# Attention and FFN kernel for one core: work moved at the FFN entries and in the three-way attention

## The reference, cut to what matters

```
# first unit, twice
x = x + 0.5 * rmsnorm(swiglu(rmsnorm(x, g0), gate0, up0, down0), g1)
x = x + rmsnorm(token_mixer(rmsnorm(x, g2)), g3)
x = x + 0.5 * rmsnorm(swiglu(rmsnorm(x, g4), gate1, up1, down1), g5)
# second unit, twice (ALPHA = sqrt(2))
mix = concat(hgrn2(x), three_way_attention(x)) @ w_out
x = layer_norm(ALPHA * x + mix)
x = layer_norm(ALPHA * x + swiglu(x, gate, up, down))
```

## Time and profile before

| | |
|---|---|
| median of 3 runs | 3692.89 us (3686.24 to 3693.57) |
| the profiled execution | 3686.6 us, its span 3684.8 us |
| TensorE busy | 3502.5 us, 95% of the span |
| VectorE busy | 1686.9 us, 46% |
| ScalarE busy | 1272.8 us, 35% |
| GpSimd busy | 1418.8 us, 39% |
| mean granted TensorE clock | 0.980 |

### The profile page before, as it was taken

One profiled execution on the slowest core, in us unless ns is written; L12 is line 12 of the kernel. 1 busy time (PEld: TensorE's weight loads), 2 busy tenths in 40 slices (PEclk: granted clock), 3 DMA queues, 4 the chain that ended last, 5 costly groups with the idle time before them and its releaser, 6 DMA issues. The chain is left out here.

```text
span 3684.8 us, 45117 instructions
## 1 busy us (share of the span) xinstructions
PE 3502.5 (95%) x16116; PEld 2751.6 (75%) x16116; DVE 1686.9 (46%) x2604; ACT 1272.8 (35%) x2154; POOL 1418.8 (39%) x605
## 2 busy tenths in 40 slices
PE   7999999899989999999999999899999899889998
PEld 5888766688868887766788777557888777568886
DVE  5442344644244423255543346854331539753323
ACT  3222346422232223355222352453222442642223
POOL 3444321244434443322444434403444345124443
PEclk9999999999999999999999999999999999999999
DMA  4223311222222323211223231102323320112222
GB/s 150 97 96 100 108 63 41 69 97 97 94 79 97 97 96 110 75 46 52 91 97 97 86 122 53 46 18 81 97 95 99 110 76 29 41 50 95 95 96 98
DMA packets 86356, 307.15 MB, mean 83 GB/s; under 512 B 11173, under 2 KB 11813, under 8 KB 84942
## 3 DMA queue, kind: packets, MB, share of 16 engines
q1 hardware_dynamic: 86222, 305.38, 25.1%
HBM read 301.13 MB, written 4.21 MB: 83 GB/s over the span
## 5 line engine op out<-in xcount | busy, mean ns | idle before, releaser
L319 POOL TENSOR_TENSOR wL<-ring,wH 128x1024 fp32r<-128x1024 f32 (+1 forms) x525 | 1280.7, 2439 | 2147.3 <-ACT wH L309 2147.3
L273 PE MATMUL bank<-hH,wH 128*128 128x512 f32 x2448 | 966.7, 395 | 18.8 <-DVE guL L645 7.9
L275 PE MATMUL bank<-hH,wL 128*128 128x512 f32 x2448 | 954.3, 390 | 0.0
L274 PE MATMUL bank<-hL,wH 128*128 128x512 f32 x2448 | 954.0, 390 | 0.0
L309 ACT ACTIVATE wH<-ring 128x1024 fp32r<-128x1024 f32 (+1 forms) x525 | 551.0, 1050 | 1125.0 <-PE bank L275 945.0
L273 PEld LDWEIGHTS bank<-hH,wH 128*128 128x128 f32 x2448 | 460.3, 188 | 122.4 <-POOL wL L319 9.6
L275 PEld LDWEIGHTS bank<-hH,wL 128*128 128x128 f32 x2448 | 460.2, 188 | 97.2
L274 PEld LDWEIGHTS bank<-hL,wH 128*128 128x128 f32 x2448 | 460.7, 188 | 95.2 <-issue 2.4
L273 PE MATMUL bank<-guH,wH 128*128 128x512 f32 x1248 | 492.5, 395 | 2.3 <-ACT early L1141 1.4
L275 PE MATMUL bank<-guH,wL 128*128 128x512 f32 x1248 | 486.9, 390 | 0.0
L274 PE MATMUL bank<-guL,wH 128*128 128x512 f32 x1056 | 410.8, 389 | 0.0
(11 more groups left out here) (287 smaller groups left out, 4089.2 us busy)
## 6 DMA issues: line engine op xcount, KB each, us to landing
ring<-in_w SPq DMA_DIRECT2D x376, 512.0 KB, 3.3
ring<-in_down SPq DMA_DIRECT2D x96, 448.0 KB, 3.1
ring<-in_down SPq DMA_DIRECT2D x48, 512.0 KB, 3.3
ring<-in_next SPq DMA_DIRECT2D x16, 512.0 KB, 3.2
mix<-in_table SPq DMA_DIRECT2D x2, 2560.0 KB
mix<-bias SPq DMA_DIRECT2D x4, 768.0 KB, 5.6
ring<-in_vg SPq DMA_DIRECT2D x8, 280.0 KB, 2.9
xT<-in_xT SPq DMA_DIRECT2D x4, 512.0 KB, 6.6
```

Of the source, the lines that this page charges most:

```text
L273: eng.matmul(out, a, hi, start=first, stop=False)
L274: eng.matmul(out, a, lo, start=False, stop=False)
L275: return eng.matmul(out, b, hi, start=False, stop=last)
L319: eng.tensor_tensor(l[:, 0:width], ring[:, n % NSLOT, 0:width], h[:, 0:width], ALU.subtract).then_inc(w_lo, 1)
```

## The change

Three things change.

First, the fourth slot's low part at the first unit's stage entries (slot n0+3 of both FFNs and of the projections) goes from GpSimd to VectorE, behind the sum of squares (`vector_lo`, the old `third_lo`; the set `by_vector` takes GpSimd's part out). Second, `act_silu` makes the high part of slot n0+4 ahead of the root and of the Silu table, where it stood behind the first `silu`; and `hi` waits for the slot that really had its buffer (`buffer_before`), where it waited for the slot two before. This holds for the FFN of the second unit too. Third, in the three-way attention tile 0 of the out projection is taken and its mean made at step 1 (was 2), tile 1 is multiplied at step 2 (was 3), and `dve_early2` is cut in two: the scaling stays ahead of `post`, the centring and adding up (`dve_early2_mid`) go behind it.

```
+        by_vector = set()
+        def buffer_before(n):
+            n -= NSLOT
+            while n in spares or n in ahead:
+                n -= NSLOT
+            return n
...
         def hi(eng, n, width=WIDE, i=0, per=0):
...
-            if per or (n >= NSLOT and n not in spares and n not in ahead):
+            if per:
                 eng.wait_ge(slots_done, i * per + (n - NSLOT + 1))
+            elif n not in spares and n not in ahead and buffer_before(n) >= 0:
+                eng.wait_ge(slots_done, buffer_before(n) + 1)
...
         def lo(eng, n, width=WIDE, i=0, per=0):
-            if n >= total_slots[0] or per == 0 and n in spares and n > 2:
+            if n >= total_slots[0] or per == 0 and n in by_vector:
                 return
-            if per == 0 and n - 1 in spares and n > 3:
+            if per == 0 and n - 1 in by_vector:
                 eng.wait_ge(w_lo, n)
...
             hi(eng, n0 + 3)
+            hi(eng, n0 + 4)
             if stat is not None:
                 act_root(eng, stat, EPS_RMS)
             eng.preload_act_table(ACT.Silu)
-            for k in range(2):
-                silu(k)
-                hi(eng, n0 + 4 + k)
+            silu(0)
+            silu(1)
+            hi(eng, n0 + 5)
...
+        by_vector.update((3, n_in + 2, n_in + 3, n_ffn1 + 2, n_ffn1 + 3, n_next + 2))
...
                     sum_x_squares(dve, 0)
+                    vector_lo(dve, 3)
...
                     sum_x_squares(dve, 1)
+                    vector_lo(dve, n_in + 3)
...
                     sum_x_squares(dve, 2)
+                    vector_lo(dve, n_ffn1 + 3)
...
-                if u == 2:
+                if u == 1:
                     eng.wait_ge(early_out, 1)
                     eng.matmul(bank[7][:, :], onesD, early2(0), start=True, stop=True).then_inc(mean_out, 1)
...
-        EARLY2_AT = (3, 6, 7, 10, 11, 14, 15)
+        EARLY2_AT = (2, 6, 7, 10, 11, 14, 15)
...
         def dve_early2(eng, m):
...
-            if m == 0:
-                return
+
+        def dve_early2_mid(eng, m):
+
             if m == 1:
                 eng.wait_ge(mean_kept, 1)
...
-                if u == 2:
-                    dve_early2(eng, 0)
                 if u - 2 in EARLY2_AT:
                     dve_early2(eng, EARLY2_AT.index(u - 2) + 1)
                 if 1 <= u <= NU:
                     post(u - 1)
+                if u == 1:
+                    dve_early2(eng, 0)
+                if u - 2 in EARLY2_AT:
+                    dve_early2_mid(eng, EARLY2_AT.index(u - 2) + 1)
...
+                if u == 2:
+                    act_guess(eng)
                 if 1 <= u <= NU:
                     back(u - 1)
-                if u == 3:
-                    act_guess(eng)
```

More of the change, by code:

```diff
@@ L420, in moved, with vector_lo @@
                 eng.tensor_scalar(xT[:, m, :], yT[:, m, :], b[:, m:m + 1], None, ALU.add).then_inc(x_ready, 1)
-        def third_lo(eng, n):
+        def vector_lo(eng, n):
             eng.wait_ge(w_hi, n + 1)
@@ L440, in dve_post @@
                     rest(eng, h0, m - 1, gains)
-            third_lo(eng, third)
+            vector_lo(eng, third)
         def pair_of(eng, n, h0, banks=(0, 2)):
@@ L2329, in build @@
         spares.update((2, n_ffn2 + 2, n_next2 + 2))
+        by_vector.clear()
+        by_vector.update((n_ffn2 + 2, n_next2 + 2))
         ahead.clear()
```

## The result

The changed kernel takes 3668.72 us (median of 6 runs, 3667.52 to 3671.4), the kernel before 3688.29 us beside it (6 runs, 3685.26 to 3693.57). The ratio is 0.9948, 95% interval 0.9938 to 0.9958: 19.6 us or 0.52% faster. The forecast was 3681 us within 3673 to 3690, a gain of 10.3 us.

What follows compares the result with a forecast made beforehand. TensorE, busy for 95% of the span, was taken as the bound, so only its stops could be won: FFN entries 5.9 us plus attention 4.4 us gave 10.3 us, and 3681 us was forecast, range 3673 to 3690.

Steps and rivals of the forecast that it cites:

- FFN entries, 5.9 us: First unit's four FFN entries: TensorE's 7.9 us stop behind the first gate result shrinks; 6.7 us gained less 0.8.
- 0.55 us late: FFN entries: VectorE's added low part ends at about 709.87, while slot n0+3 began at 709.34, so that slot starts later.
- The 0.8 us set aside for L1376: Two first FFN entries: GpSimd's part may come ahead of L1376, delaying the gates; 0.8 us taken between nothing and 2.0.
- The landing that a rival spoke of: FFN entries of both units: slot n0+4's late load holds ScalarE ahead of the root; slower, 3699 us, chance 0.05.
- The reduction: Rival: without GpSimd's low part beside it the reduction shortens, up to 2.4 us in five of six places; 3669 us, chance 0.03.
- The second unit's entries: High part of slot n0+4 ahead of the table moves the first `silu` 3.5 us later, covered by TensorE's slots; cost zero.
- The loop's start, 0.3 us a layer lost: Attention steps 1 to 4: score reads 2.25 us late, TensorE level after turn 2 and tile 1, 0.3 us lost at step 4.
- the race that the prediction left open: Attention step 4, `post(4)` against GpSimd's low part: VectorE first wins 1.05 us, GpSimd first loses 0.5; 0.3 lost taken.
- The cut, 2.5 us a layer: Three-way attention: cutting `dve_early2` brings `post` 1.4 us sooner at steps 7, 11 and 15; gain 2.5 us per layer.
- the three waits behind `post`, 2.7 us: Attention: TensorE waits at `turn_cmp` for `post` three times per layer, 2.7 us together, the longest 1.6.
- theory C: From the follow-up runs' expectations: much of the gain is granted clock; entries alone 8 to 12 us less, attention alone 10 to 14.

Runs made afterwards that it cites:

- the second profile: The changed kernel run once more, unaltered, beside the kernel before: 3671.88 us, ratio 0.9954; its profiled execution took 3675.0 us.
- e1: Kernel before with the FFN entries part alone (high part of slot n0+4 early, low part of n0+3 on VectorE), attention as before: 3679.51 us, ratio 0.9974.
- e3: Kernel before with only the high part of slot n0+4 ahead of the root; low part of n0+3 stays on GpSimd: 3679.67 us, ratio 0.9974.
- e9: The changed kernel without the shift of the attention's start, so the entries part and the cut, against the kernel before: 3663.16 us, ratio 0.9932.
- e4: Kernel before with only the low part of slot n0+3 on VectorE; high part of n0+4 stays behind the first `silu`: 3688.1 us, ratio 0.9997.
- e5: Kernel before with only the cut of `dve_early2`; mean, tile 1 and guess at their old steps: 3670.0 us, ratio 0.9954.
- e10: Kernel before with the cut, tile 0's sum behind `post(0)`, mean at step 1, guess at step 2, tile 1 left at step 3: 3682.78 us, ratio 0.999.
- e8: The changed kernel with the attention's third streamed slot's high part at step 3 in place of step 4: 3672.57 us, ratio 0.9956 to the kernel before.

## Why the prediction was too small

**FFN entries, 5.9 us: right in mechanism, a little small.** The windows give 6.5 (71.7 to 65.2, in five profiles with this part 64.7 to 65.5). The two second entries won 1.83 and 1.89 us in place of 1.58. The working took slot n0+3 to be 0.55 us late, by the start of its first matmul. It starts 0.55 us later against the start of the window (709.34 - 701.53 = 7.81 before, 710.14 - 701.78 = 8.36 now), but the first matmul had taken 0.80 us before and takes 0.50 now (why it was slow no run shows); the slot's last starts only 0.30 us later (13.45 and 13.75). Layer 1's first entry won 2.5 us here and 1.9 in the second profile, where 1.97 were expected. The 0.8 us set aside for L1376 did not come: at layer 1's first entry VectorE was first by 0.08 us.

```profile
1086.81 0.23 DVE L1389 TENSOR_TENSOR small<-small 128x64 f32<-128x64 f32 x1
...
1086.89 2.41 POOL L329 TENSOR_TENSOR wL<-ring,wH 128x1024 fp32r<-128x1024 f32 x1 [32.42 <-DVE wL L437]
```

Layer 0's first entry gave 0.3 us in this profile and 1.4 in six others with this part (24.1 against 25.5). The landing that a rival spoke of is late there: the high part of slot n0+4 waits for it, and the root starts 18.69 us into the window in place of 18.06.

```profile
46.95 1.06 ACT L319 ACTIVATE wH<-ring 128x1024 fp32r<-128x1024 f32 x1 [7.30 <-DMA ring<-in_w]
47.91 0.58 ACT L389 ACTIVATE work<-bank 128x512 f32<-128x512 f32 x1
```

That costs little, since the slot ahead is late by as much. What ate the gain in the one profile is the clock. By a window over slot n0+3's beginning:

```profile
47.70:51.10 3.40, 3.40 (x10) 0.50 0.48 154
```

The granted clock is at the lower of its two levels (1.2 GHz), TensorE just back from its wait of 1.62 us for the reduction, and ten matmuls take 3.4 us where they take 2.3 otherwise (0.23 each). In e1, e3 and e9 such a stretch lies in this window too (granted 0.93), but ahead of the reduction's end, where TensorE would have waited anyway.

In the second entry above the landing was in time: 2.7 us lie between the end of the copy (706.27) and the root's matmul (709.01). The medians give the entries more than the windows do: 8.3 us, 9.9 at equal clock, with an interval that reaches down to 5.9. Where the difference would lie no window shows, and it stays open.

**The reduction** takes 7.41 us as before, though GpSimd is silent beside it: that rival is out. It had priced the change at 3669 us, and the measured 3668.7 meets that number by luck alone. **The second unit's entries** went as said: the first `silu` starts 5.8 us behind slot n0+2's first matmul (2517.33 - 2511.53) in place of 2.1, 3.7 us later, and TensorE has no wait behind it.

**The loop's start, 0.3 us a layer lost: right.** From the turn of step 1, `turn(1, WIN)` comes 6.69 us later (2364.24 - 2357.55) against 4.14 before, 2.5 us late where 2.3 were expected, after waits of 1.25 and 1.05 us. Behind turn 2 and tile 1 TensorE is level, as the chain had it: 12.7 us from the turn of step 1 (2370.26 - 2357.55) where 12.8 were expected. At step 4 the race that the prediction left open went to GpSimd, by 0.11 us:

```profile
2376.40 2.35 POOL L329 TENSOR_TENSOR wL<-ring,wH 128x1024 fp32r<-128x1024 f32 x1 [20.20 <-ACT wH L319]
2376.51 2.27 DVE L2092 TENSOR_TENSOR mix<-mix 128x6 f32<-128x6 f32 x1
```

`turn(4, SLC)` starts 21.69 us from the turn of step 1 in place of 21.08: 0.6 us lost, where the prediction had 0.5 for this case. By the windows with the same clock on both sides the start lost 0.35 us (30.55 to 30.90) and 0.6 (28.87 to 29.48 in the second profile).

**The cut, 2.5 us a layer: this step failed, by its size.** The later windows fall from 72.87 and 74.55 to 69.48 and 69.49. Over all profiles they are 74.1 us on average without the cut (12 windows, 72.8 to 75.4) and 69.4 with it (16 windows, 68.3 to 70.2): 4.7 us a layer. The working took the three waits behind `post`, 2.7 us, from one profile, and put nothing for the clock. The groups of TensorE from step 5 on in the second layer, with the busy time and then the idle time ahead of them; before:

```profile
L1925 PE MATMUL bank<-mats,mix 128*128 128x128 f32 x110 | 18.1, 296 | 3.5 <-ACT mix L2144 2.9 <-DVE mix L2087 0.5
...
L1932 PE MATMUL bank<-mats,mix 128*128 128x128 f32 x6 | 1.3, 301 | 2.7 <-DVE mix L2082 2.7
```

e4, with the same attention:

```profile
L1939 PE MATMUL bank<-mats,mix 128*128 128x128 f32 x110 | 17.4, 288 | 4.6 <-ACT mix L2158 4.2 <-DVE mix L2101 0.3
...
L1946 PE MATMUL bank<-mats,mix 128*128 128x128 f32 x6 | 1.3, 301 | 3.2 <-DVE mix L2096 3.2
```

With the cut (e5) the two groups have 3.7 and 0.0. So the mechanism was right: the waits of `turn_cmp` go, and those of `turn` stay near what they were before. But the waits that the working read differ from one execution to the next, 6.2 us in the one row pair and 7.8 in the other. TensorE was idle for 6.5 us in each of the two later windows of the profile before, and for 7.8 to 9.5 in the ten of the other kernels without the cut. The difference lies at step 13. Its score matmuls ran at the lower level of the clock in the first layer before (granted 0.58 over 2454.24 to 2458.0), and at full clock in e4:

```profile
2454.24 3.93 PE L1915 MATMUL bank<-mix 64*128 64x31 f32 x12
```

```profile
2456.32 2.54 PE L1929 MATMUL bank<-mix 64*128 64x31 f32 x12
...
2461.04 0.68 PE L1939 MATMUL bank<-mats,mix 128*128 128x128 f32 x4 [1.59 <-ACT mix L2158]
```

A wait of 0.35 us stood behind the first, one of 1.59 behind the second: TensorE was slower by 1.4 us and waited 1.2 us less. So part of the wait was hidden in a longer matmul. One window with the cut, the second layer of e10, has these matmuls at full clock:

```profile
3233.66 2.54 PE L1915 MATMUL bank<-mix 64*128 64x31 f32 x12
...
3238.39 0.68 PE L1925 MATMUL bank<-mats,mix 128*128 128x128 f32 x4 [1.59 <-ACT mix L2147]
```

The wait of 1.59 us is the same as without the cut, so the cut does not shorten it. What it shortens there is `turn_cmp`: 0.7 us in place of e4's 3.2, which is the 2.5 us of the prediction.

What was left out is where the stretch at half clock lies. With the stretch at step 13 on both sides, in the first layer before, in e5 and in the changed kernel, the window falls from 72.87 to 69.65 and 69.48, by 3.2 to 3.4 us: 2.5 to 2.8 of idle time, and 0.6 to 0.7 of TensorE's busy time, which no row explains. Where the stretch comes behind step 13, as in e4 (74.13), the window is 1.3 us longer than before's. Without the cut the stretch covers step 13 in 5 of 12 windows, with the cut in 15 of 16 (there the matmuls take 3.6 to 4.2 us and the wait is 0.35 or less). Whether the cut brings that about or chance does, no run separates. In the second layer the kernel before had one such stretch more, at step 15 (granted 0.53 over 3245.66 to 3249.08, and TensorE's busy time 68.06 against 66.39 us), which makes 1.7 of the 5.1 us there.

Sum of the shown parts: entries 6.5, cut 2 x 4.7, start 2 x -0.5: 14.9 us, against 16.9 at equal clock and 19.6 and 15.3 by the two pairs of medians. Some 2 us remain unplaced. The mean granted clock, on which the working was silent, has its share in the single numbers (the changed kernel's first runs had 0.9817 on average, the second ones 0.9806, some 2 us apart by the slope), but it isn't the cause of the gain: theory C, a change that wins through a higher mean clock, is out, since 16.9 us remain at equal clock.

**Two sums in the prediction** are off, and bear on nothing that came: the mean of its four times is 3689.8, not 3690.1, and the rival of a late landing, 28 us dearer than the forecast of 3681, would be 3709 us, not 3699.

**What the prediction did not ask.** It took the cut to work at steps 7, 11 and 15, and step 4's wait to be settled by the shift. The cut alone removes that wait at its old place. The shift does so too, by itself; and put together, they undo it: tile 1's additions, now behind `post(3)` at step 4, stand ahead of the reads of step 5, `post(4)` comes 0.11 us behind GpSimd's part, and the early mean has added its 2.3 us. With the same clock on both sides, the loop's start takes 27.5 and 26.2 us in e9, 30.9 and 29.5 in the changed kernel's two profiles: 3.3 to 3.4 us a layer. The change as made left 6.5 us of its own gain behind at equal clock (3670.6 against 3664.1), and 5.6 and 8.7 by the two pairs of medians.

## What to carry to other kernels

Where a change has two edits that aim at one wait, price each alone before both: here either removes the wait, and together they bring it back. One profile gives one phase of the clock, and its list of waits is that execution's alone. Look at whether the matmuls ahead of a short wait ran at half clock: the wait may be longer in the next execution, here 1.59 us in place of 0.35. And work that nobody waits for belongs behind work that somebody does, the more so where another engine's long operation may hold whichever comes next.

## What the hardware showed beside

GpSimd's low part holds more than the two-input operations that the prediction's sums had in view: one of VectorE's scalings with a single operand in SBUF took 2.58 us beside it (L2103 in e8), 0.48 us being what 128x512 of it takes otherwise. The reduction was not held (7.41 us with GpSimd's part beside it and without, 7.49 beside two). GpSimd is held in its turn: in e5 its part began 0.04 us behind VectorE's L2018 (2383.88, 0.68 us) and took 2.87 us in place of 2.4. So a planned meeting can't be avoided by ordering one- and two-input operations alone.

The Trainium skill covers this by two pages read together. GPSIMD Engine Reference (Specifications) names two cases of contention, two SBUF inputs and a two-port mode; VectorE: DVE Perf Modes says that a tensor_scalar on SBUF can use both read ports for its one tensor and a tensor_tensor can't (Mode 2×_2P), and gives the former twice the latter's rate in fp32 too (The perf-mode tier table). The traces agree as far as they go: 0.48 us for a 128x512 scaling against 0.69 for a two-input operation of that size, and these two kinds were seen held and the reduction was not. A held operation stood until GpSimd's whole part was over: in the changed kernel L2092 ended at 2378.78, GpSimd's part at 2378.75.

The same kernel on the same data had a mean granted clock of 0.979 and 0.982 in two executions, 6.5 us apart. What a stretch at half clock costs hangs on where it lies: on a slot with nothing to wait for behind it, as at 47.70, a microsecond; on matmuls ahead of a wait for another engine, as at 2454.24, 1.4 us of stretched work cost 0.1 (4.86 us from the first score matmul to the turn behind the wait, against 4.72 in e4).
